# Weighing the gathered experts in twos instead of fours, the first two between TensorE's second and third spread

## The reference

```
q = (xb @ w_query).reshape(PEER_BLOCK, PEER_HEADS, 2, D_HALF)
s = jnp.einsum('thpd,hpkd->thpk', q, sub_keys,
...
sv, si = lax.top_k(s, PEER_TOPK)
...
u = expert_u[eidx]
a = jnp.einsum('thkd,td->thk', u, xb, preferred_element_type=jnp.float32)
w = (g * jax.nn.gelu(a, approximate=False)).astype(xb.dtype)
return jnp.einsum('thk,thkd->td', w, expert_v[eidx])
```

## Time and profile before

| what | before |
|---|---|
| median of 3 runs | 3683.89 us (3681.74 to 3687.78) |
| the profiled execution | 3686.14 us, its span 3684.3 us |
| mean granted TensorE clock | 0.985 |
| PE busy | 3158.2 us (86%) |
| PEld busy (weight loads, beside PE) | 1389.9 us (38%) |
| DVE busy | 2311.1 us (63%) |
| ACT busy | 719.1 us (20%) |
| POOL busy | 1110.6 us (30%) |
| gathers' queue (q0) | 1208.03 MB, 79.4% of the 16 DMA engines' span |
| Gelu of a four (L861), mean of 288 | 207 ns |

### The profile page before, as it was taken

How to read it: one execution, slowest core, us unless ns; L and a number is a source line. 1 busy time by engine, 2 the same in 40 slices (tenths; PEclk the granted TensorE clock), 3 DMA queues, 4 the chain that set the end, 5 groups by cost and what they waited for, 6 DMA issues and landing times.

```text
span 3684.3 us, 48012 instructions
## 1 busy us (share of the span) xinstructions
PE 3158.2 (86%) x17895; PEld 1389.9 (38%) x17895; DVE 2311.1 (63%) x6107; ACT 719.1 (20%) x2373; POOL 1110.6 (30%) x1177
## 2 busy tenths in 40 slices
PE   6999999889888878988887898889788888977776
PEld 3545556634334324423432343344234334422222
DVE  1333343867757866775776677677667757765444
ACT  2434434311111111111111111111111111111111
POOL 0000000033333333333333333333333333333332
PEclk8999999799999999999999999999999999999999
DMA  5000114299999999999999999999999999999997
GB/s 217 24 29 23 35 34 169 91 401 421 421 421 419 418 414 417 413 414 420 415 414 420 416 414 415 417 418 416 412 417 416 416 416 418 413 414 420 419 418 326
DMA packets 192682, 1275.60 MB, mean 346 GB/s; under 512 B 21056, under 2 KB 24768, under 8 KB 44608
## 3 DMA queue, kind: packets, MB, share of 16 engines
q0 software_dynamic: 165888, 1208.03, 79.4%
q1 hardware_dynamic: 26560, 64.49, 4.9%
HBM read 1260.12 MB, written 12.32 MB: 345 GB/s over the span
## 4 chain that ended last, share of the span: by engine, by line
DMA 46%; PE 35%; DVE 9%; issue 5%; POOL 4%; ACT 1%; SPq 0%; DVEq 0%; POOLq 0%; ACTq 0%
DMA arena<-in_experts,arena 45%; PE PS L1353 10%; PE PS L1182 8%; PE PS L1367 7%; POOL arena L651 4%; DVE arena L976 4%; PE PS L1276 3%; PE PS L1166 2%; PE PS L1399 2%; PE PS L1265 1%; PE PS L1225 1%; DVE arena L1051 1%; DVE arena L1054 1%; DVE arena L1057 1%; PE PS L1205 0%
## 5 line engine op out<-in xcount | busy, mean ns | idle before, releaser
L1353 PE MATMUL PS<-arena 128*128 128x512 bf16 x6912 | 1655.6, 382 | 453.1 <-DVE arena L976 440.6
L976 DVE CUSTOM_DVE_ANT_0 arena<-arena,PS 128x1024 f32<-128x1024 f32 x1152 | 1396.2, 1221 | 871.7 <-DMA arena<-in_experts,arena 548.4
L651 POOL DMA_INDIRECT arena<-in_experts,arena x1152 | 1089.0, 945 | 1938.0 <-PE PS L1367 1572.7
L1353 PEld LDWEIGHTS PS<-arena 128*128 128x128 bf16 x6912 | 611.5, 98 | 1480.5 <-DVE arena L976 865.1
L1367 PE MATMUL PS<-arena 128*32 128x512 f32 x4608 | 558.8, 603 | 16.8 <-ACT arena L867 16.8
L861 ACT ACTIVATE arena<-arena 128x4 f32<-128x4 f32 x288 | 59.5, 207 | 2156.2 <-DVE arena L976 2137.0
L1182 PE MATMUL PS<-arena 128*128 128x512 f32 (+1 forms) x720 | 309.8, 567 | 13.9 <-DMA arena<-in_w_in 7.9
L1399 PEld LDWEIGHTS PS<-arena 128*128 128x128 f32 x2304 | 266.6, 192 | 101.5 <-issue 101.5
L1399 PE MATMUL PS<-arena 128*128 128x128 f32 x2304 | 289.7, 280 | 0.0
L867 ACT ACTIVATE arena<-arena 128x1 f32<-128x1 f32 x1152 | 245.5, 284 | 9.4
L1367 PEld LDWEIGHTS PS<-arena 128*32 128x32 f32 x4608 | 120.8, 109 | 313.9 <-issue 175.4
(11 more groups left out here) (124 smaller groups left out, 1526.8 us busy)
## 6 DMA issues: line engine op xcount, KB each, us to landing
arena<-in_experts,arena POOLq DMA_INDIRECT x1152
arena<-in_w_in SPq DMA_DIRECT2D x8, 1024.0 KB, 11.8
arena<-in_w_query SPq DMA_DIRECT2D x4, 2048.0 KB, 16.1
arena<-in_xT SPq DMA_DIRECT2D x9, 512.0 KB, 3.9
h_scratch<-arena SPq DMA_DIRECT2D x9, 512.0 KB, 2.9
arena<-h_scratch SPq DMA_DIRECT2D x9, 512.0 KB, 8.1
out<-arena SPq DMA_DIRECT2D x9, 512.0 KB
arena<-in_x_prompt SPq DMA_DIRECT2D x8, 512.0 KB, 3.5
```

The source lines that it names most:

```text
L651: pool.indirect_dma_start(out=uv[r], out_offset=None, in_=experts, in_offset=bass.IndirectOffsetOnAxis(ap=expert_T[t % 2][:, tok:tok + 1], ...
L976: dve.tensor_tensor_reduce(uv[r][:, 0:D], uv[r][:, 0:D], xb(n), 1.0, 0.0, ALU.mult, ALU.add, a_dot[(n // 4) % 2][:, n % 4:n % 4 + 1]).then ...
L1353: mm = pe.matmul(PS[:, 2 + 2 * (n % 2) + c, :], pick[:, tok:tok + 1].broadcast_to([P, P]), parts[t % 2][k][:, 512 * c:512 * c + 512], star ...
```

## The change

The eight weighing matmuls of a four are issued as two halves. `weigh_experts(n, q)` now takes the blocks 2q and 2q+1 of the four, for both halves of the outputs. The first half stands between the four's second and third spread, the second where both stood. ScalarE does Gelu and two weights for each two blocks (`pair`), and each half of TensorE's work counts `two_used` up, which takes the place of `four_used` with everyone who waits: GpSimd's gathers wait in twos. Number and shapes of the matmuls stay the same.

```diff
@@ GpSimd
-                        if n >= RING and (n - RING) % 4 == 0:
-                            pool.wait_ge(four_used, (n - RING) // 4 + 1)
+                        if n >= RING and (n - RING) % 2 == 0:
+                            pool.wait_ge(two_used, (n - RING) // 2 + 1)
@@ ScalarE
-                        act.wait_ge(dots_ready, 4 * n + 4)
-                        act.activation(a_gelu[n % 2], a_dot[n % 2], ACT.Gelu).then_inc(gelu_ready, 1)
-                        act.wait_ge(gelu_ready, n + 1)
-                        if n >= 2:
-                            act.wait_ge(four_used, n - 1)
-                        for g in range(4):
-                            tok = 32 * g + f
-                            act.activation(wz[n % 2][:, g, 31:32], a_gelu[n % 2][:, g:g + 1], ACT.Copy,
-                                           scale=gate_T[t % 2][:, tok:tok + 1]).then_inc(wgt_ready, 1)
+                        for q in range(2):
+                            pair = slice(2 * q, 2 * q + 2)
+                            act.wait_ge(dots_ready, 4 * n + 2 * q + 2)
+                            act.activation(a_gelu[n % 2][:, pair], a_dot[n % 2][:, pair], ACT.Gelu).then_inc(gelu_ready, 1)
+                            act.wait_ge(gelu_ready, 2 * n + q + 1)
+                            if n >= 2:
+                                act.wait_ge(two_used, 2 * n + q - 3)
+                            for g in range(2 * q, 2 * q + 2):
+                                tok = 32 * g + f
+                                act.activation(wz[n % 2][:, g, 31:32], a_gelu[n % 2][:, g:g + 1], ACT.Copy,
+                                               scale=gate_T[t % 2][:, tok:tok + 1]).then_inc(wgt_ready, 1)
@@ VectorE
-                        dve.wait_ge(gelu_ready, n // 4 - 1)
+                        dve.wait_ge(gelu_ready, 2 * (n // 4) - 2)
-                    dve.wait_ge(four_used, FOURS * (t + 1))
+                    dve.wait_ge(two_used, 2 * FOURS * (t + 1))
@@ TensorE
-                def weigh_experts(n, c):
+                def weigh_experts(n, q):
                     t, f = n // FOURS, n % FOURS
-                    if c == 0:
-                        pe.wait_ge(wgt_ready, 4 * n + 4)
+                    pe.wait_ge(wgt_ready, 4 * n + 2 * q + 2)
+                    if q == 0:
                         if f == 0 and t:
                             pe.wait_ge(acc_free, t)
                         if n == 0:
                             pe.wait_ge(h_ready, 4 * NT)
-                    for g in range(4):
-                        r = (4 * n + g) % RING
-                        mm = pe.matmul(PS[32 * g:32 * g + 32, ACC + c, :], wz[n % 2][:, g, 31 - f:63 - f],
-                                       uv[r][:, D + 512 * c:D + 512 * c + 512], start=(f == 0), stop=(f == FOURS - 1))
-                    if c == 1:
-                        mm.then_inc(four_used, 1)
+                    for c in range(2):
+                        for g in range(2 * q, 2 * q + 2):
+                            r = (4 * n + g) % RING
+                            mm = pe.matmul(PS[32 * g:32 * g + 32, ACC + c, :], wz[n % 2][:, g, 31 - f:63 - f],
+                                           uv[r][:, D + 512 * c:D + 512 * c + 512], start=(f == 0), stop=(f == FOURS - 1))
+                    mm.then_inc(two_used, 1)
@@ TensorE's order
                         spread_x(4 * n + 2)
                         spread_x(4 * n + 3)
+                        weigh_experts(n, 0)
                         spread_x(4 * n + 4)
                         spread_x(4 * n + 5)
-                        weigh_experts(n, 0)
                         weigh_experts(n, 1)
```

More of the change, by code:

```diff
@@ L461, in build @@
         wgt_ready = sem("wgt_ready")
-        four_used = sem("four_used")
+        two_used = sem("two_used")
         acc_free = sem("acc_free")
```

## The result

The change made the kernel slower: 3736.27 us median (3735.36 to 3737.28, 4 runs) against 3682.81 us (3680.68 to 3687.78, 4 runs), a ratio of 1.014 with a 95% interval of 1.0129 to 1.0152. The forecast was 3734 us, between 3698 and 3785.

What follows compares the result with a forecast made beforehand. DMA gathers set the pace at 324.6 us a tile; dearer halves put TensorE at 329. Tiles 1 to 7 +31, tile 0 +14, unevenness +6, less 1: +50 us on 3683.89, 3734 us, range 3698 to 3785.

Steps and rivals of the forecast that it cites:

- What bounds: Late stage: gathers set the pace at 324.6 us a tile; TensorE changes matter only once its work passes that.
- The half's price: Weighing on TensorE: each half costs a whole's 1.85 us plus 0.10 for entering column groups, 1.95 more for each four.
- unevenness: Fours 0 to 18, with routing: lag of 15 us exceeds 12 of slack; about 0.8 us a tile, +6.
- Tile 0: First tile: TensorE needs 325.8 us from 759.2, less 2.6 plus about 3, ending at about 1085.5: +14 us.
- The stall at squares: Four 4 of a tile: TensorE waits 3.1 us for weights behind ScalarE's squares and table load.
- What early freeing buys: GpSimd's gathers in twos: about 5 us more slack each, some 12 in all; in itself this buys nothing.
- The Trainium skill's rule: A pack spans one matmul plus some 4 ns per further tile; without switching price, 1.7 us a half, +6 us.
- Half price: Rival, chance 0.07: two groups stream in half the time, a tile needs 274.5 us and the time stays at 3682.
- the absorbing ring: Rival, chance 0.08: halves at full price but switches overlap, so only tile 0 pays: 3690 to 3700 us.
- the deeper queue: Rival, chance 0.03: blocks land at 2.48 instead of 2.536 us, up to 60 us gained, if halves come cheap.
- Halves of 2.05 us or more: Rival, chance 0.08: TensorE binds harder because halves are this long, total over 3785 us.
- waves alone: Lower bound on the half's price: 1.71 us without switching, about +6 us, 3690 us.

Runs made afterwards that it cites:

- both halves last: The changed kernel with both halves after the fourth spread, so nothing stands between the second and third; 3682.91 us, ratio 0.9998 to the kernel before.
- squares moved: The changed kernel with ScalarE's squares at four 4 behind the first pair's weights instead of ahead of them; 3705.72 us, ratio 1.0056 to the kernel before.
- four-wide halves: The changed kernel with each half filling four column groups, output columns 512 to 1023 going to the two left empty; 3682.95 us.
- block by block: The kernel before with the weighing's two loops swapped, both output halves of a block one after the other; 3685.27 us, ratio 1.0003.

## Why the prediction was right, step by step

**What bounds.** The DMA set the pace with TensorE close behind, and it took only a larger need of TensorE to turn this. Shown from both sides: more TensorE time for the weighing gives 3736 and 4243 us; the same dear halves beside cheaper spreads give 3686.

**The half's price.** 1.95 us was forecast, 1.85 and 0.10 for entering. Measured: 1.84 to the next instruction, and from two spreads' start to the half's 2.68 (1904.59 back to 1901.90 for the spreads), 0.09 more than their 2.59. The number held, and the picture behind it held only for halves that stand apart. (The 0.453 us of L1276 that it was compared with is for one of the two records of such a matmul, as is the 0.43 of a wave.) I argued from waves that all groups take in step; the runs showed lists that each group works off by itself. For the forecast it made no difference, as the change puts spreads between the halves. For "both halves last" it made one of 50 us.

**The terms of the sum.** Starts of the dots of block 128 and block 1024, before:

```profile
1067.90 1.22 DVE L976 CUSTOM_DVE_ANT_0 arena<-arena,PS 128x1024 f32<-128x1024 f32 x1 [1.24 <-issue]
```

```profile
3349.15 1.22 DVE L976 CUSTOM_DVE_ANT_0 arena<-arena,PS 128x1024 f32<-128x1024 f32 x1 [1.24 <-issue]
```

and after:

```profile
1079.44 1.22 DVE L978 CUSTOM_DVE_ANT_0 arena<-arena,PS 128x1024 f32<-128x1024 f32 x1 [1.24 <-PE PS L1355]
```

```profile
3399.53 1.22 DVE L978 CUSTOM_DVE_ANT_0 arena<-arena,PS 128x1024 f32<-128x1024 f32 x1 [1.24 <-issue]
```

| stretch (profiled executions) | before | after | difference | forecast |
|---|---|---|---|---|
| to dot 128 | 1067.9 | 1079.4 | +11.5 | +14 |
| dot 128 to dot 1024, tiles 1 to 7 | 2281.3 | 2320.1 | +38.8 | +37 (31 and 6 of unevenness) |
| dot 1024 to the last dot (3668.6, 3719.9) | 319.5 | 320.4 | +0.9 | 0 |
| last dot to the end of the span | 15.7 | 13.6 | -2.1 | -1 with the start |
| span | 3684.3 | 3733.5 | +49.2 | +50 |

A middle tile takes 331.4 us (2320.1 / 7); TensorE's need was put at 329 and unevenness at 0.8, together 329.7. Before it took 325.9 (2281.3 / 7), where the forecast had 324.6: that was a mean over 800 to 3600 us, with parts of tile 0 and of the last tile, whose dots come every 2.50 and 2.51 us, while those of tiles 1 to 7 come every 2.546. Both values were low, by 1.7 and 1.3 us, and it is luck that in the difference, 5.5 against 5.2 a tile, they nearly cancel.

The medians differ by 53.5 us, 4 more than these two executions: the profiled one of before (3686.14) lay 3.3 above its median and the one after (3735.36) 0.9 below. The forecast's base was 3683.89, where the four executions give 3682.81.

**Tile 0** came out 2.5 us below the forecast because this execution reached the expert layer earlier: ScalarE's norm of the next tile starts at 753.13 instead of 755.64, and the first half with it at 756.68 instead of the 759.2 that I had. What the tile itself cost is the 14 us that were forecast.

**The stall at squares.** 3.1 us a tile was forecast from rows 10; the timeline after, at four 4 of tile 1, ahead of the late half that is shown above:

```profile
1127.22 2.75 PE L1355 MATMUL PS<-arena 128*128 128x512 bf16 x12
...
1127.90 1.06 ACT L795 ACTIVATE arena<-arena 128x1024 f32<-128x1024 f32 x1
...
1130.68 1.28 ACT L863 ACT_TABLE_LOAD   x1
```

TensorE waits 2.77 us for the weights behind Gelu's table load, which the squares make necessary. The wait was right and its size near. What the forecast left out is the clock behind it: the half after the wait runs at 0.50 and takes 1.6 us more, so the stall costs 4.4 us a tile.

**Unevenness.** Its 0.8 us a tile stood for losses of the DMA while the ring is dry, in the fours with routing. There is nothing of the kind there: in the run with squares moved, fours 0 to 18 take 204.5 us in every tile, which is the sum's 19 x 9.08 + 32. What is left over its 325.8 a tile, 1.3 us, lies in fours 19 to 31: some 122.3 us against TensorE's own 121. (The forecast's 118 for them leaves out the 3.1 of routing at fours 30 and 31.) Over half of it is one place, at four 23, where a spread waits 0.7 us for a dot that VectorE starts late, behind its selection; the prediction had named this as a cause. So two terms were wrong, the stall by 1.3 and the unevenness by 0.5, both to the low side.

**What early freeing buys.** "In itself this buys nothing" was right with the DMA as the bound (four-wide halves: 3682.95). Under the change's own conditions it kept 27 us. The prediction had the cause, 12 us of slack instead of 7, and no price for it.

**The Trainium skill's rule** (TensorE: Matmul & The Clock Gate, Part 3), that a pack spans one matmul's duration plus some 4 ns for each further tile, agrees with 1.90 us for one block's four records and 1.91 for two blocks' eight. The same part says that matmuls start and end in program order. Two runs here don't: both halves last (1.87 us instead of 3.67) and block by block (3685 us instead of about 4200).

**The rivals.** Half price fell with the timeline (1.84 us a half), the absorbing ring with tile 1 to 7's +38.8 us, the deeper queue with the four-wide halves, where it had its best chance and the time is that of before. Halves of 2.05 us or more fell with 1.84 + 0.09, and waves alone, 1.71 us without any price for switching, with the same number.

## What to carry to other kernels

Matmuls on column groups are paid by the longest list of one group between two pieces of whole-array work. Before such a pack is split so that something can start earlier, see that each part still fills all groups, or that nothing for the whole array comes between the parts: the same 4608 records cost 559, 621 or 1114 us here. And where an engine stands just below the one that sets the pace, add up its need from start-to-start distances: 263 + 66 = 329 us a tile came close to the 331 measured, where busy time (276 + 66 = 342) would have made the loss four times the size. When such an engine is made to wait, count what comes after the wait too: here 2.77 us of waiting cost 4.4, as the next half ran at half the clock.

## What the runs showed of the hardware that I had not expected

- Column groups take their fp32 records independently, out of the program's order: two halves of two groups each in 1.87 us, and a block-by-block order at no cost (563.3 us of busy time as against 558.8).
- One 128x128 spread between two halves is enough to part them: 1.84 us each.
- Behind a wait of 2.77 us at squares the granted clock was 0.50: the half there took 3.37 to 3.53 us instead of 1.84, in each of seven tiles.
- At the end the last weighing got faster. Before:

```profile
3671.02 3.64 PE L1367 MATMUL PS<-arena 128*32 128x512 f32 x16 [4.59 <-ACT arena L867]
```

after, the last half:

```profile
3721.92 1.91 PE L1370 MATMUL PS<-arena 128*32 128x512 f32 x8 [2.37 <-ACT arena L869]
```

The granted clock was 0.50 in the stretch of the first (3671 to 3675) and 1.00 in that of the second (3721.9 to 3723.9). In the 7 us ahead of it TensorE was at work for 2.20 us in the kernel before (3664 to 3671), with the last 4.59 us idle, and for 4.42 us after the change (3714.9 to 3721.9), with the first half of that four among them and the last 2.37 us idle. That is 1.7 of the 2.1 us that the end gained.
